# A two-layer hybrid decoder trunk: down product by column quarters, scatter in four row tiles, another order of the expert loads, other ends of the layers

## The chip, the cores and the metric

One Trainium2 chip, of which the kernel uses one core. The metric is the device time of one execution in microseconds (us), lower is better.

## The reference, cut to what matters

x is 256 tokens by 1024 features, float32. Each of two layers does a mixer and a mixture of experts (MoE), each on a normed input and added back. The change touches the MoE part, and the last norm.

```python
for layer in range(2):
    h = h + mixer(rms_norm(h, mix_norm))             # even: MoBA + RetNet heads; odd: dilated windows
    h = h + hier_moe(rms_norm(h, ffn_norm[layer]), ...)
return rms_norm(h, final_norm)

def hier_moe(h, ...):                                # 32 experts, 4 groups, top-1 group, top-2 inside it
    hid = jax.nn.silu(xb @ w_gate[e]) * (xb @ w_up[e])    # w_gate[e], w_up[e]: 1024 x 512
    y = hid @ w_down[e]                                    # w_down[e]: 512 x 1024
    out = zeros((n_tok, d)).at[row_tok].add(y * row_gate[:, None])
```

Every expert is computed: 3 matrices of 2 MB each, 32 experts, 2 layers. With the mixers' weights the kernel reads 439.72 MB.

## The kernel before, in words

**Memory.** `ring` holds ten units of 2 MB, filled by SyncE's queue (SP) alone. Four pairs of units (`PAIR_AT`) hold gate and up weights, two (`DOWN_AT`, units 9 and 6) down weights. During a layer's mixer the units hold the blocks of the input projection (0 to 5), and unit 6 the split weights (`split`), 7 the keys (`kT`), 8 the queries (`qT`) and `h_high`, 9 and 6 the output projection (`W_OUT_AT`).

**The MoE stage.** Expert e has 32 slots. I call its steps on TensorE G(e), D(e), S(e). `gather` brings the tokens of four experts to their slots with one-hot matmuls. `gate_up` (L836, G) makes 32 matmuls of 256 columns on four column tiles into bank 6. ScalarE takes the exponential and a copy, VectorE does `hidden` (L1267: SiLU, product, transpose to `hidT`). `down` (L855, D) turns the gates, then makes 8 matmuls of 512 columns: column tile j holds the product of hidden features j, so the four partial products stand in four groups of 32 partitions of banks 4 and 5. ScalarE copies bank 4 (L603) and VectorE bank 5 (L1293) to `y_sb`. `scatter` (L873, S) is 4 full matmuls of 512 columns, which add the partial products, weight them and add them to the four accumulator banks 0 to 3. `start_sums` puts h into these banks.

**Order.** TensorE runs, for each expert e: G(e+2), D(e), S(e), and after S of every second expert of a group `gather` for the next group. Groups of four experts, seven of them in a loop, the last one behind it as code of its own. (A further round for experts with more than 32 tokens stands between, under an `If`.) SP runs `load_group` (L401): wait for G(e), load pair e+4 (P(e+4)), wait for D(e), load down weights e+2 (W(e+2)). The queue is in order, so P(e+5) is asked for only when D(e) is done.

**Between the layers.** After the last scatter ScalarE and VectorE copy h back, TensorE turns it (`turn_h`), ScalarE and VectorE split it in a high and a low part (`split_hT`, `split_columns`), and `project` begins with the weights that `split_chunks` has split.

**The end.** After the last scatter, per token tile t: squares on ScalarE (L724), variance on VectorE, power on GpSimd, one Newton step, two multiplications with gain (L1401), output DMA.

## Time and profile before

| | |
|---|---|
| runs | 1209.9, 1211.75, 1213.74 us; median 1211.75 |
| profiled execution | 1207.12 us; its span 1204.7 us |
| TensorE busy | 980.2 us (81%) |
| VectorE, ScalarE, GpSimd busy | 420.7, 231.0, 36.9 us |
| DMA | 441.34 MB, mean 366 GB/s |
| the chain that ended last | DMA 43%, PE 41%, DVE 9%, ACT 3%, issue 2% |

PE is TensorE, PEld its weight loads, DVE VectorE, ACT ScalarE, POOL GpSimd, SPq the queue of SyncE. A float32 matmul stands in the trace as two records, so "x8" is four matmuls. Times in a timeline are us from the start of the span. "[1.85 <-DVE ...]" is the idle time of the engine before the row and what ended it.

### The profile page before, as it was taken

The numbers are of one execution on the slowest core, as the hardware profiler recorded it, in microseconds if no ns is written. First come the engines' busy times: TensorE is split into PE (matmuls) and PEld (weight loads), VectorE is DVE, ScalarE is ACT, GpSimd is POOL, SyncE is SP. The second block draws the span as 40 slices with busy tenths as digits, with TensorE's granted clock in tenths as the row PEclk, the third lists the DMA queues.
The fourth block names the chain that finished last, engine by engine and source line by source line (L and its number), as shares of the span: only waits on it lengthen the run. The fifth ranks groups of instructions, "written<-read, shape, count | busy, mean of one in ns | idle before, by whom it ended". The sixth has DMA issues, their size and how long they took to land.

```text
span 1204.7 us, 18458 instructions
## 1 busy us (share of the span) xinstructions
PE 980.2 (81%) x7528; PEld 535.0 (44%) x7528; DVE 420.7 (35%) x1073; ACT 231.0 (19%) x553; POOL 36.9 (3%) x52
## 2 busy tenths in 40 slices
PE   8998998878787768676899999888877768777865
PEld 6874544434342424342378656344343434343422
DVE  6774533232222222222278735322322222222222
ACT  5643111010000000000255630101100000000001
POOL 1002000000000000000010210000000000000000
PEclk9999999998999999998999998999999999899999
DMA  9976369999999999999895543799999999999993
GB/s 359 304 283 271 140 272 428 430 427 428 429 429 429 428 428 429 429 428 424 341 338 232 223 163 135 302 428 427 429 429 429 427 428 430 429 428 427 430 425 160
DMA packets 50681, 441.34 MB, mean 366 GB/s; under 512 B 8784, under 2 KB 8784, under 8 KB 25936
## 3 DMA queue, kind: packets, MB, share of 16 engines
q1 hardware_dynamic: 50496, 440.26, 88.2%
q8 instruction: 27, 0.44, 0.1%
q10 hardware_dynamic: 144, 0.52, 0.1%
q14 instruction: 14, 0.11, 0.0%
HBM read 439.72 MB, written 1.05 MB: 366 GB/s over the span
## 4 chain that ended last, share of the span: by engine, by line
DMA 43%; PE 41%; DVE 9%; ACT 3%; issue 2%; SPq 1%; POOL 1%; DVEq 0%; ACTq 0%
DMA ring<-in_w_expert_up 32%; PE bank L848 12%; DMA ring<-in_w_expert_down 11%; PE bank L880 6%; PE bank L905 4%; PE bank L867 3%; PE bank L756 3%; PE bank L758 3%; PE bank L757 3%; PE bank L830 2%; DVE work L1273 1%; DVE work L1293 1%; PE bank L733 1%; PE bank L938 1%; DVE split L1073 1%
## 5 line engine op out<-in xcount | busy, mean ns | idle before, releaser
L848 PE MATMUL bank<-ring,work 128*32 128x256 f32 x4096 | 264.4, 415 | 82.2 <-DMA ring<-in_w_expert_up 71.4
L880 PE MATMUL bank<-work 128*128 128x512 f32 x512 | 235.0, 601 | 95.6 <-DVE work L1293 95.6
L848 PEld LDWEIGHTS bank<-ring,work 128*32 128x32 f32 x4096 | 146.5, 119 | 209.2 <-issue 108.6
L1272 DVE TENSOR_SCALAR work<-work 128x128 f32<-128x128 f32 x64 | 14.5, 227 | 538.3 <-ACT work L596 538.3
L880 PEld LDWEIGHTS bank<-work 128*128 128x128 f32 x512 | 92.0, 189 | 243.7 <-issue 243.7
L595 ACT ACTIVATE work<-bank 128x128 f32<-128x128 f32 x64 | 17.8, 278 | 684.4 <-PE bank L848 684.4
L867 PE MATMUL bank<-ring,work 128*32 128x512 f32 x1024 | 123.1, 598 | 16.1 <-DMA ring<-in_w_expert_down 16.1
L756 PE MATMUL bank<-split,h_high 128*128 128x512 f32 x192 | 77.2, 402 | 6.8 <-DVE split L1073 3.4
L1073 DVE SCALAR_TENSOR_TENSOR split<-ring,gains,split 128x512 fp32r<-128x512 f32 x96 | 68.0, 748 | 24.1 <-ACT split L635 23.4
L758 PE MATMUL bank<-split,h_high 128*128 128x512 f32 x192 | 75.0, 391 | 0.0
L757 PE MATMUL bank<-split,h_low 128*128 128x512 f32 x192 | 74.9, 390 | 0.0
L635 ACT ACTIVATE split<-ring,gains 128x512 fp32r<-128x512 f32 x96 | 65.9, 720 | 28.0 <-PE bank L758 27.5
L830 PEld LDWEIGHTS bank<-work,xn 128*128 128x128 f32 x512 | 59.5, 192 | 9.1 <-issue 9.1
L1273 DVE RECIPROCAL work<-work 128x128 f32<-128x128 f32 x64 | 61.0, 953 | 2.2
L830 PE MATMUL bank<-work,xn 128*128 128x128 f32 x512 | 59.9, 275 | 0.8 <-DVE work L1245 0.8
L603 ACT COPY work<-bank 128x512 f32<-128x512 f32 x64 | 37.5, 586 | 105.5 <-PE bank L867 105.5
L905 PE MATMUL bank<-ring,hT 128*128 128x512 f32 x128 | 57.1, 596 | 0.0
L867 PEld LDWEIGHTS bank<-ring,work 128*32 128x32 f32 x1024 | 27.6, 109 | 65.8 <-issue 56.0
L1262 DVE TENSOR_TENSOR work<-bank,gains 128x512 f32<-128x512 f32 x32 | 22.1, 691 | 96.2 <-PE bank L830 96.2
L1293 DVE COPY work<-bank 128x512 f32<-128x512 f32 x64 | 43.8, 685 | 23.8 <-PE bank L867 23.8
L756 PEld LDWEIGHTS bank<-split,h_high 128*128 128x128 f32 x192 | 36.0, 188 | 17.3 <-DVE h_low L1065 6.2
L758 PEld LDWEIGHTS bank<-split,h_high 128*128 128x128 f32 x192 | 36.0, 188 | 7.9
(144 smaller groups left out, 691.8 us busy)
## 6 DMA issues: line engine op xcount, KB each, us to landing
ring<-in_w_expert_gate SPq DMA_DIRECT2D x64, 2048.0 KB, 30.6
ring<-in_w_expert_up SPq DMA_DIRECT2D x64, 2048.0 KB, 35.0
ring<-in_w_expert_down SPq DMA_DIRECT2D x64, 2048.0 KB, 26.3
ring<-in_w_in_even SPq DMA_DIRECT2D x5, 2048.0 KB, 18.3
ring<-in_w_in_odd SPq DMA_DIRECT2D x5, 2048.0 KB, 20.9
ring<-in_w_out_even SPq DMA_DIRECT2D x2, 2048.0 KB, 8.6
ring<-in_w_out_odd SPq DMA_DIRECT2D x2, 2048.0 KB, 14.3
ring<-in_w_in_even SPq DMA_DIRECT2D x2, 1024.0 KB, 8.2
```

Source lines behind the costliest of these rows:

```text
L635: act.activation(w_high[u % PARTS], ring[:, j, 512 * c:512 * c + 512], ACT.Copy, scale=gains[:, 2 * l, c:c + 1]).then_inc(w_high_ready, 1)
L756: pe.matmul(bank, high, wh, start=(c == 0), stop=False)
L757: pe.matmul(bank, low, wh, start=False, stop=False)
L758: last = pe.matmul(bank, high, wl, start=False, stop=(c == C - 1))
L830: last = pe.matmul(psum[4 + c // 4][:, P * (c % 4):P * (c % 4) + P], xn_c[:, t, c, :], onehot[:, t, :, :].rearrange("p k s -> p (k s)"), s ...
L848: last = pe.matmul(psum[6][32 * j:32 * j + 32, 0:2 * P].rearrange("p (a s) -> p a s", a=2), xT[:, c, SLOTS * k:SLOTS * k + SLOTS], ring[:, ...
L867: last = pe.matmul(psum[4 + half][32 * j:32 * j + 32, :], hidT[k][:, 32 * j:32 * j + 32], ring[:, DOWN_AT[k % 2], D * j + 512 * half:D * j ...
L880: pe.matmul(acc[t][half][:, :], gatedT[:, P * t:P * t + P], y_sb[:, 512 * half:512 * half + 512], start=False, stop=last).then_inc(scatter ...
L905: last = pe.matmul(mix_bank(n, t)[:, :], oT[:, c, P * t:P * t + P], ring[:, W_OUT_AT[n], 512 * c:512 * c + 512], start=(c == MIX_ORDER[l][ ...
L1073: dve.scalar_tensor_tensor(out=w_low[u % PARTS], in0=ring[:, j, 512 * c:512 * c + 512], scalar=gains[:, 2 * l, c:c + 1], in1=w_high[u % PA ...
L1273: chain.link(dve.reciprocal(eb, eb))
L1293: dve.tensor_copy(y_sb[:, 512:1024], psum[5][:, :]).then_inc(y_high[l], 1)
```

## The change

The down product: all four tiles q hold the same hidden features j in turn and add over j in the bank; tile q makes output columns 256q to 256q+255. So y is 128 partitions by 256 columns (32 slots for each quarter), in bank 4 alone. ScalarE alone copies it. The scatter makes 8 matmuls of 256 columns, each with 32 rows of the array (`tile_position=(32 * q, 0)`), quarter q into bank q. `gather` stands ahead of the scatter. `start_sums` stands ahead of the MoE stage, in the place of three warm-up matmuls, and no longer between G(1) and G(2). SP asks for P(4) and P(5) first, then W(2), W(3), and then in the old order. Units change: split weights in 7, keys in 6, second half of the output projection in 7; the loads before the MoE stage follow. Between the layers the first two chunks of layer 1's weights are split before the wait for the last scatter, h is copied back in quarters once both token tiles are done, and turned through banks 4 to 7. At the end both token tiles go together.

```diff
-W_OUT_AT = DOWN_AT
+W_OUT_AT = (9, 7)
+SPLIT_AT, KT_AT, QT_AT = 7, 6, 8
+QUARTER = D // 4
...
-        y_sb = work[:, 4096:5120]
-        acc = [[psum[2 * (1 - t) + half] for half in range(2)] for t in range(T)]
+        y_sb = work[:, 4096:4352]
+        acc = [psum[q][:, :].rearrange("p (t n) -> p t n", t=T) for q in range(4)]
...
-                load_pair(l, l * EXPERTS + GE - 1, GE - 1)
-                for k in range(2):
-                    sp.wait_ge(mixed[l], T * (k + 1))
-                    load_down(l, l * EXPERTS + k, k)
+                sp.dma_start(ring[:, unit + 1, :], up_rows[row]).then_inc(pair_arrived[l][GE - 1], 16)
+                load_down(l, l * EXPERTS + 1, 1)
+                sp.wait_ge(mixed[l], T)
+                load_down(l, l * EXPERTS, 0)
+                sp.wait_ge(mixed[l], T * 2)
+                sp.dma_start(ring[:, unit, :], gate_rows[row]).then_inc(pair_arrived[l][GE - 1], 16)
...
-                with sp.Fori(0, GROUPS_OF - 1) as g:
-                    load_group(l, 0, g)
+                for e in range(2):
+                    next_pair(l, e, e + GE, e)
+                for e in range(2):
+                    next_down(l, e, e + AHEAD, e)
+                load_rest(l, 0)
...
+            def load_rest(l, r):
+                with sp.Fori(0, GROUPS_OF - 2) as g:
+                    for k in range(GE):
+                        e = GE * g + AHEAD + k
+                        next_pair(l, r * EXPERTS + e, GE * g + (AHEAD + GE + k), (AHEAD + k) % GE)
+                        next_down(l, r * EXPERTS + e, GE * g + (2 * AHEAD + k), k % 2)
+                for e in range(EXPERTS - 6, EXPERTS - 4):
+                    next_pair(l, r * EXPERTS + e, e + 4, e % GE)
+                    next_down(l, r * EXPERTS + e, e + 2, e % 2)
...
-                act.copy(y_sb[:, 0:512], psum[4][:, :]).then_inc(y_low[l], 1)
+                act.copy(y_sb, psum[4][:, 0:QUARTER]).then_inc(y_ready[l], 1)
...
-                for half in range(2):
-                    for j in range(4):
+                for j in range(4):
+                    for q in range(4):
                         last = pe.matmul(
-                            psum[4 + half][32 * j:32 * j + 32, :], hidT[k][:, 32 * j:32 * j + 32],
-                            ring[:, DOWN_AT[k % 2], D * j + 512 * half:D * j + 512 * half + 512],
-                            start=True, stop=True, tile_position=(0, 32 * j))
+                            psum[4][32 * q:32 * q + 32, 0:QUARTER], hidT[k][:, 32 * j:32 * j + 32],
+                            ring[:, DOWN_AT[k % 2], D * j + QUARTER * q:D * j + QUARTER * q + QUARTER],
+                            start=(j == 0), stop=(j == 3), tile_position=(0, 32 * q))
...
                 for t in range(T):
-                    for half in range(2):
-                        pe.matmul(acc[t][half][:, :], gatedT[:, P * t:P * t + P], y_sb[:, 512 * half:512 * half + 512],
-                                  start=False, stop=last).then_inc(scattered[l], 1)
+                    for q in range(4):
+                        rows = slice(32 * q, 32 * q + 32)
+                        last = pe.matmul(acc[q][:, t, :], gatedT[rows, P * t:P * t + P], y_sb[rows, :],
+                                         start=False, stop=last_expert and t == T - 1, tile_position=(32 * q, 0))
+                last.then_inc(scattered[l], 1)
...
                     down(l, r, g, k)
-                    scatter(l, expert_no(r, g, k), not after and k == GE - 1)
                     if k == GE - AHEAD - 1 and after:
+                        pe.wait_ge(y_ready[l], e + 1)
                         gather(l, group_no(*after))
+                    scatter(l, e, not after and k == GE - 1)
...
-                keep_warm(2, cst[:, 0:512])
+                for q in range(2):
+                    start_sums(q)
...
-                keep_warm(1, cst[:, 0:512])
+                for q in range(2, 4):
+                    start_sums(q)
...
-                start_sums(l)
...
+                if l < LAYERS - 1:
+                    act.wait_ge(gain_loaded[2 * l + 2], 16)
+                    split_chunks(l + 1, 0, 0, AHEAD)
+                act.wait_ge(scattered[l], (more + 1) * EXPERTS)
+                if l < LAYERS - 1:
+                    for q in range(2):
+                        act.copy(h[:, :, QUARTER * q:QUARTER * q + QUARTER], acc[q]).then_inc(h_left_back, 1)
+                else:
+                    for q in range(4):
+                        if q >= 2:
+                            act.wait_ge(gained, q - 1)
+                        for t in range(T):
+                            act.activation(h[:, t, QUARTER * q:QUARTER * q + QUARTER], acc[q][:, t, :],
+                                           ACT.Square, accum_out=sq4[:, t, q:q + 1]).then_inc(squared, 1)
+                    act.wait_ge(rstd_ready, T * (2 * LAYERS + 1))
+                    act.wait_ge(gained, 4)
+                    act.activation(xn_t[:, 0, :], xn_t[:, 0, :], ACT.Copy, scale=rstd[:, 0:1]).then_inc(out_ready[0], 1)
```

VectorE likewise splits two chunks and copies quarters 2 and 3 of h; at the end it multiplies each quarter with the gain (`gained`), adds the eight sums, does one Newton step for both tiles, and scales tile 1.

## Rows read from the trace of the kernel before

**Rows 1.** The page: 40 slices of the span, in tenths.

```profile
PEclk9999999998999999998999998999999999899999
DMA  9976369999999999999895543799999999999993
```

**Rows 2.** The page's costliest groups: busy us, mean ns of one; idle before.

```profile
L848 PE MATMUL bank<-ring,work 128*32 128x256 f32 x4096 | 264.4, 415 | 82.2 <-DMA ring<-in_w_expert_up 71.4
L880 PE MATMUL bank<-work 128*128 128x512 f32 x512 | 235.0, 601 | 95.6 <-DVE work L1293 95.6
```

**Rows 3.** Windows: both MoE starts; last columns are granted clock, DMA share, GB/s.

```profile
165.00:170.00 5.00, 4.53 (x62) 1.75 (x54) 1.82 (x5) 1.22 (x4) 0.00 (x0) 1.00 0.51 216
170.00:175.00 5.00, 3.60 (x8) 1.44 (x9) 1.25 (x3) 0.18 (x1) 0.00 (x0) 1.00 0.86 308
...
765.00:770.00 5.00, 4.80 (x66) 1.92 (x58) 1.60 (x4) 0.95 (x4) 0.00 (x0) 1.00 0.57 242
770.00:775.00 5.00, 3.34 (x8) 1.44 (x8) 1.48 (x4) 0.45 (x1) 0.00 (x0) 1.00 0.81 279
```

**Rows 4.** Timeline of the SP queue, layer 0's second request (W(2)).

```profile
169.73 0.33 SPq L384 DMA_DIRECT2D ring<-in_w_expert_down  x1
```

**Rows 5.** Timeline of TensorE, start of layer 0's MoE stage.

```profile
142.95 3.66 PE L733 MATMUL bank<-cst 128*128 128x512 f32 x4
...
148.36 3.81 PE L830 MATMUL bank<-work,xn 128*128 128x128 f32 x32 [0.45 <-DVE work L1245]
...
160.01 3.70 PE L887 MATMUL bank<-h,cst 128*128 128x512 f32 x8
163.64 3.66 PE L848 MATMUL bank<-ring,work 128*32 128x256 f32 x64
```

**Rows 6.** Timeline of TensorE, last experts of layer 0.

```profile
558.16 1.57 PE L848 MATMUL bank<-ring,work 128*32 128x256 f32 x18 [3.86 <-issue]
563.64 4.05 PE L848 MATMUL bank<-ring,work 128*32 128x256 f32 x46 [3.91 <-issue]
...
571.75 3.67 PE L880 MATMUL bank<-work 128*128 128x512 f32 x8 [1.83 <-DVE work L1293]
...
579.31 1.92 PE L867 MATMUL bank<-ring,work 128*32 128x512 f32 x16
...
596.39 3.67 PE L880 MATMUL bank<-work 128*128 128x512 f32 x8 [0.91 <-DVE work L1293]
```

**Rows 7.** Timeline of TensorE, layer 1: one wait in the loop, then its end.

```profile
1111.75 5.35 PE L848 MATMUL bank<-ring,work 128*32 128x256 f32 x64 [3.36 <-DMA ring<-in_w_expert_up]
...
1162.18 1.50 PE L848 MATMUL bank<-ring,work 128*32 128x256 f32 x24 [1.66 <-issue]
...
1192.40 3.67 PE L880 MATMUL bank<-work 128*128 128x512 f32 x8 [0.91 <-DVE work L1293]
```

**Rows 8.** The chain: start, us; P(30) of layer 0 and of layer 1.

```profile
519.89 35.95 DMA ring<-in_w_expert_up
...
1120.53 35.33 DMA ring<-in_w_expert_up
```

**Rows 9.** DMA issues at 581 to 582 us (W(31), first half block); us to landing.

```profile
ring<-in_w_expert_down SPq DMA_DIRECT2D x1, 2048.0 KB, 7.9
ring<-in_w_in_odd SPq DMA_DIRECT2D x1, 1024.0 KB, 10.2
```

**Rows 10.** Timelines of ScalarE and VectorE: copy to gatedT, between the layers, the end.

```profile
568.25 0.39 ACT L601 COPY work<-bank 128x256 f32<-128x256 f32 x1
...
599.72 2.56 ACT L635 ACTIVATE split<-ring,gains 128x512 fp32r<-128x512 f32 x4
...
602.79 2.48 DVE L1065 TENSOR_TENSOR h_low<-bank,h_high 128x512 fp32r<-128x512 f32 x4 [0.68 <-ACT h_high L617]
...
1200.28 1.41 DVE L1401 SCALAR_TENSOR_TENSOR xn<-bank,small,hT 128x512 f32<-128x512 f32 x2
```

More of the change, by code:

```diff
@@ L292, in build @@
         squared = sem("squared")
+        gained = sem("gained")
+        out_ready = sems("out_ready", T)
         var_ready = sem("var_ready")
@@ L422, in load_w_out @@
+            def load_across(l, r):
+                for k in range(6):
+                    next_pair(l, r * EXPERTS + k - GE, k, k % GE)
+                    next_down(l, r * EXPERTS + k - GE, EXPERTS - AHEAD + k if k < AHEAD else k - AHEAD, k % 2)
             def load_w_out(l, n):
@@ L871, in down, with scatter @@
                 last.then_inc(down_done[l], 1)
-            def scatter(l, e, last):
+            def scatter(l, e, last_expert):
                 pe.wait_ge(gatedT_ready[l], e + 1)
-                pe.wait_ge(y_low[l], e + 1)
-                pe.wait_ge(y_high[l], e + 1)
+                pe.wait_ge(y_ready[l], e + 1)
                 for t in range(T):
-                    for half in range(2):
-                        pe.matmul(acc[t][half][:, :], gatedT[:, P * t:P * t + P], y_sb[:, 512 * half:512 * half + 512],
-                                  start=False, stop=last).then_inc(scattered[l], 1)
@@ L883, in start_sums @@
-            def start_sums(l):
-                for t in range(T):
-                    for half in range(2):
-                        pe.matmul(acc[t][half][:, :], ident, h[:, t, 512 * half:512 * half + 512],
-                                  start=True, stop=False).then_inc(scattered[l], 1)
+                    for q in range(4):
+                        rows = slice(32 * q, 32 * q + 32)
+                        last = pe.matmul(acc[q][:, t, :], gatedT[rows, P * t:P * t + P], y_sb[rows, :],
+                                         start=False, stop=last_expert and t == T - 1, tile_position=(32 * q, 0))
@@ L890, in group, with start_sums @@
+                last.then_inc(scattered[l], 1)
+            def start_sums(q):
+                pe.matmul(acc[q], ident, h[:, :, QUARTER * q:QUARTER * q + QUARTER], start=True, stop=False)
             def group(l, r, g, after):
                 for k in range(GE):
+                    e = expert_no(r, g, k)
                     if k < GE - AHEAD:
@@ L1298, in group @@
                         choose_slots(l, group_no(*after), GE * after[1])
+                    if k < GE - AHEAD or after:
+                        hidden(l, e + AHEAD, ahead)
+                    if k == GE - AHEAD - 1 and after:
                         columns(l, group_no(*after))
@@ new lines, in _ @@
+                    split_chunks(l + 1, 0, 0, AHEAD)
+                dve.wait_ge(scattered[l], (more + 1) * EXPERTS)
+                if l < LAYERS - 1:
+                    for q in range(2, 4):
+                        dve.tensor_copy(h[:, :, QUARTER * q:QUARTER * q + QUARTER], acc[q]).then_inc(h_right_back, 1)
+            link = norm_link
+            squares = 4 * 2 * LAYERS
+            dve.wait_ge(fin_loaded, 16)
+            for q in (2, 3, 0, 1):
+                if q < 2:
+                    dve.wait_ge(squared, squares + T * (q + 1))
+                cols = slice(QUARTER * q, QUARTER * q + QUARTER)
+                dve.tensor_tensor(xn_t[:, :, cols], acc[q], gain_row[:, cols].unsqueeze(1).broadcast_to([P, T, QUARTER]),
+                                  ALU.mult).then_inc(gained, 1)
```

118 lines of the change are left out of this document (52 added, 66 removed).

## The prediction

> **What bounds the kernel now.** I read the page first. The row of the DMA engines stands at 9 tenths in both MoE stages, while PE's share is lower there than in the mixers [rows 1]. The costliest groups then say how PE waits: G, the largest, had 71.4 us of idle time ended by the DMA of up weights, but S 95.6 us by VectorE's copy of y [rows 2]. The reader should see two kinds of time in this. While the DMA queue is full, an expert costs its bytes: three transfers of 2048 KB are 6.29 MB, at about 429 GB/s [rows 1] 14.7 us, whatever PE does. PE needs less: G 3.64 us (its row less the overlap with the next), the gates' turn 0.37, D 1.90, the wait 1.83, S 3.67, and a quarter of a gather of 3.8 [rows 5, 6], together 12.4. So the 235 us of S are mostly slack. What PE does sets the time in three places alone: (a) where the queue runs dry after a MoE stage's start, (b) from the last pairs' landing to the stage's end, (c) behind the last scatter. The mixers, from `project` to the gather, are untouched but for loads that move.
>
> **(a) The start.** The windows show the hole: behind P(4) the 16 DMA engines move 216 and then 308 GB/s, in layer 1 242 and 279 [rows 3]. Against 429 this is 2.5 + 1.4 = 3.9 us without data, in layer 1 2.2 + 1.7 = 3.9. It ends when W(2) is asked for at 169.73 us [rows 4], since SP waits for D(0) before it looks at G(1). After the change P(5) is asked for when G(1) ends, at about 160.0 us, where now `start_sums` begins [rows 5]. P(4) transfers for 9.8 us, until about 167.5, so the hole closes; W(2) is then asked for at about 167 (G(2), turn, D(0) without the 3.70 of `start_sums` ahead), and P(5) covers until 177. The stream gains 3.9 us in each layer. The price: four matmuls of 0.92 us replace three of warm-up ahead of the gather, one more, of which the gather's idle 0.45 us [rows 5] hides half. +0.5. Net -3.4 us on every landing of the stage. Waits of SP further on have the old order, the landing order of P and W at the end is unchanged. The moved loads at the end of a mixer have the same bytes behind the same waits, except gate(3), which is asked for last; G(3) comes after some 20 us, so nothing.
>
> **The steps of an expert.** D: 16 matmuls of 256 columns on four tiles. G makes 32 of these in 3.64 us, so 1.82, against 1.90 [rows 5, 6]: I keep 1.90. The wait between D and S: VectorE's `hidden` and copy are out of it, what is left is ScalarE's copy of 256 columns, 0.39 us [rows 10], with its handing over 0.63, against 1.83 (0.91 where no `hidden` stands ahead [rows 6, 7]). S: eight matmuls of 256 columns and 32 rows. No row tiles are in the trace. Lower bound: G's rate on column tiles, 0.114 us each, 0.91. Upper bound: no overlap, eight times 0.46, 3.67 as now. A middle one: a weight load of 128 columns with its matmul record comes every 0.12 us in the gather (32 in 3.81 us [rows 5]), 16 of them 1.9. I take 1.3, between the ends that the overlap on column tiles makes likely.
>
> The Trainium skill (TensorE: Matmul & The Clock Gate, packing of small matmuls) gives 3.07 times for four row tiles of 512 columns, which would make S 3.67 / 3.07 = 1.2 us, an estimate from that page, and the sum below 0.2 us better; no row here shows it.
>
> **(b) The end of layer 0's stage.** Before: P(30) lands at 555.8 [rows 8], P(31) three transfers later, 570.6, W(29) one more, 575.4. G(30) runs 558.2 to 567.7, 6.2 us of it stalled as "issue" behind the loop's exit [rows 6]; D(28) ends at 569.9, S(28) at 575.4, D(29) at 581.2, S(31) at 600.1. After, step by step: P(30) 552.4, G(30) ends 564.3 with the same stalls, D(28) 566.6, S(28) 566.6 + 0.63 + 1.3 = 568.5 (P(31) is there since 567.2), G(31) 572.1, D(29) 574.4. Now W(31), asked for at 574.5, is what is late next: before it took 7.9 us [rows 9], and 600 us was far behind. It lands at 582.4 (W(30) at 576.9, S(30) over by 580.8). D(31) 584.3, S(31) 584.3 + 0.63 + 1.3 = 586.2. That is 13.9 us earlier.
>
> Then the turn to layer 1. The split of two chunks is put ahead of the wait; it needs the first half block, which lands 10.2 us after its issue [rows 9], 0.4 us after that of W(31): 585.1. ScalarE splits until 586.6 (four took 2.56 us [rows 10]), VectorE until 587.4, and copies two quarters of h by 588.8, where the scatter alone would allow 587.7. Turn of the first bank 0.6, cast 0.6, four subtractions 2.48 [rows 10] with handings over: `project` at 592.7, before 605.3. Of the 13.9 us 12.6 are left. The mixer behind it keeps its length; its blocks stand in the queue at 5.4 us each against 11.6 us of projection each.
>
> **(b) in layer 1**, in the clock of before: P(30) 1155.9 [rows 8] becomes 1152.5, G(30) with its stall of 1.66 us [rows 7] ends 1160.3 instead of 1163.7, D(28) 1162.6, S(28) 1164.5. P(31) lands at 1167.0, so PE waits; G(31) 1167.6 to 1171.2, W(29) 1171.9, D(29) 1173.9. W(31) 8.3 us later, 1182.3, D(31) 1184.2, S(31) 1186.1, before 1196.1 [rows 7]. -10.0.
>
> **(c) The end.** Before, 8.6 us from the last scatter to 1204.7: two squares 1.3, the root 2.9 with the other tile's two multiplications in it, two multiplications 1.41 [rows 10], output 3.0. After: eight squares of 256 columns 2.8; the root without the 1.41 but with sums of four, 1.8; one scaling of 1024 columns 1.05; the second output's issue 0.4 behind the first; 3.0. 9.05, so +0.5. Here the change loses; bounds 8.1 (squares at 0.25 each) to 10.1 (0.39 each).
>
> **Sum.** -12.6 - 10.0 + 0.5 = -22.1 us. Span 1204.7 to 1182.6; the execution's own time 1207.1 to 1185.0. The median of the runs is 4.6 us above the profiled one, so 1211.75 - 22.1 = 1189.6.
>
> **Rivals.**
>
> 1. *Row tiles don't overlap.* S keeps 3.67. Layer 0: S(28) 570.9, G(31) 574.5, D(29) 576.8, S(29) 581.1, D(30) 583.4, S(30) 587.7, D(31) 590.0, S(31) 594.3, and no block to wait for, so `project` at 599.8: -5.5. Layer 1 the same way: D(28) 1162.6, S(28) 1166.9, G(31) 1171.2, D(29) 1173.5, S(31) 1191.0: -5.1. With the end -10.1: 1201.6. For it: no row shows row tiles. Against: column tiles overlap fully, G at 0.114 us a matmul.
> 2. *The stream's hole or the tail gives back less*: stalls behind the loop's exit are longer (the code of a group grows by 96 matmul records and as many loads), or W(30) and W(31) land later. One stall of 3.9 us [rows 6] more in each layer, one half of it hidden by the wait for P(31) in layer 1: -16, 1195.8.
> 3. *The slow clock, the other side.* After 3.36 us of waiting G took 5.35 us instead of 3.64 [rows 7], so the clock fell to 1.2 GHz when PE waited. Now PE waits longer: an expert needs 3.64 + 0.37 + 1.90 + 0.63 + 1.3 + 0.9 = 8.7 us of 14.7, and one gap is near 6 us. If all ran at 1.2 GHz, the 8.1 us of work would double: 16.8 us, above the 14.7 of the bytes, and each of some 25 experts in each layer would cost 2.1 us more: +105 - 22, about 1295. It decides from the point where over three quarters of PE's work (6.0 of 8.1) is slow. Against it: the busier PE gets, the more clock it was granted, and down to three quarters nothing is lost in the loop. In the tail no gap is over 2.5 us. The Trainium skill (TensorE: Matmul & The Clock Gate, the HAM clock gate) says that the clock is throttled by default and activity releases it, and warns of waits between bursts. By that rule, the clock rows above agree, but the page leaves the share open.
> 4. *Nothing is gained*: the hole moves behind P(5) and S is hidden anyway, within 3.6 us. Against: the tail's 14 us of scatters stand on the chain with no cover.
>
> **How the numbers follow.** The forecast 0.63, rival 1 0.13, rival 2 0.12, rival 3 0.06, rival 4 0.06. The forecast's own range: S between 0.91 and 1.9 us moves two scatters in each layer, -1 and +2; the end ±1; the tail's waits ±2; the spread of runs ±2: 1184 to 1194. To leave out no more than 2 in 10 it must reach rivals 1 and 2: 1184 to 1202. What a measurement of this kernel can tell is about 0.3%, 3.6 us. Faster by more than that is the forecast and rivals 1 and 2, 0.88; within it rival 4, 0.05; slower rival 3 and a rest, 0.07.
>
> **What would show it.** (a) No dip below 420 GB/s in the 20 us behind the first P(4), and pairs 4 and 5 asked for 4 us apart. Scatter groups of 16 records in 0.9 to 1.8 us, 0.6 us behind D. PE idle before G for 5 to 6 us in the loop, DMA still at 427 to 430 GB/s, clock lower than 0.97 in the mean. (b) In both tails D(31) is released by the DMA of down weights, `project` starts about 12 us earlier. (c) 9 us from the last scatter to the end. The prediction is wrong if S takes 3.6 us, if the rate falls in the stages, or if D(31) waits much longer than 8 us behind D(29).

## The result, and the profile after

The changed kernel takes 1194.68 us (median of 4 runs, 1193.59 to 1195.5). The kernel before took 1210.91 us in the same job (4 runs, 1209.9 to 1213.74). The ratio is 0.9862, 95% interval 0.9842 to 0.9881: 16.2 us faster, where 22.1 were forecast. The profiled execution took 1195.5 us with a span of 1193.5, 11.2 less than before's 1204.7. The medians lie further apart than the profiles because before's profiled execution (1207.12 us) was quicker than all of its timed runs, and after's was the slowest of its four. What follows compares spans, and so explains 11.2 us against 22.1.

The page of after, 40 slices: the granted clock, the DMA share and GB/s.

```profile
PEclk9999898878787888786899998988797978787877
DMA  9967369999999999999995543899999999999994
GB/s 359 308 272 289 141 265 424 428 429 429 428 429 429 428 428 428 428 429 426 381 379 231 217 165 136 349 427 430 429 428 427 429 429 428 428 428 429 428 425 171
```

The same row of the page of before, where the 429 GB/s of the prediction stand:

```profile
GB/s 359 304 283 271 140 272 428 430 427 428 429 429 429 428 428 429 429 428 424 341 338 232 223 163 135 302 428 427 429 429 429 427 428 430 429 428 427 430 425 160
```

The rate in both MoE stages is the one of before: the bytes still set the time of the loop. The clock row is new against [rows 1]: 7 and 8 in the stages, mean 0.865 against 0.966. TensorE waits more, and is granted less. The costliest groups of after say the same of G, D and S (busy us, mean ns; idle before):

```profile
L878 PE MATMUL bank<-ring,work 128*32 128x256 f32 x4096 | 318.3, 478 | 226.6 <-DMA ring<-in_w_expert_up 208.5
...
L897 PE MATMUL bank<-ring,work 128*32 128x256 f32 x2048 | 126.1, 387 | 17.9 <-DMA ring<-in_w_expert_down 17.9
L910 PE MATMUL bank<-work 32*128 32x256 f32 x1024 | 74.3, 403 | 29.1 <-ACT work L622 29.1
```

Against [rows 2], S fell from 235.0 us to 74.3 and its wait from 95.6 to 29.1. G grew from 264.4 to 318.3 and its wait for up weights from 71.4 to 208.5. TensorE has 160.7 us less to do in S and waits 66.5 less ahead of it; of this 227 us, 191 came back as a slower G (53.9) and a longer wait for the same up weights (137.1).

**The start of layer 0.** Windows of after (columns: PE, PEld, DVE, ACT, POOL, clock, DMA share, GB/s), then SP's queue:

```profile
165.00:170.00 5.00, 4.89 (x86) 2.50 (x76) 3.60 (x11) 0.86 (x4) 0.00 (x0) 1.00 1.02 433
170.00:175.00 5.00, 4.53 (x80) 2.75 (x80) 1.39 (x4) 0.32 (x1) 0.00 (x0) 1.00 1.00 423
...
770.00:775.00 5.00, 5.00 (x68) 4.01 (x70) 1.71 (x3) 0.00 (x0) 0.00 (x0) 1.00 0.98 416
```

```profile
158.99 0.33 SPq L387 DMA_DIRECT2D ring<-in_w_expert_gate  x1
...
163.31 0.33 SPq L387 DMA_DIRECT2D ring<-in_w_expert_gate  x1
...
169.95 7.88 SPq L391 DMA_DIRECT2D ring<-in_w_expert_down  x2
```

The windows that had 216 and 308 GB/s in layer 0 and 242 and 279 in layer 1 [rows 3] have over 415. Pairs 4 and 5 are asked for 4.3 us apart. From the first gather (151.60; before 148.36 [rows 5]) to P(31)'s landing, 569.90 as the chain below has it, it is 418.3 us. Before it was 570.6 - 148.36 = 422.2. So the hole's 3.9 us are gained in full, but the gather itself started 3.2 us later.

**The end of layer 0's stage**, timeline of TensorE, and two lines of the chain:

```profile
570.03 5.35 PE L878 MATMUL bank<-ring,work 128*32 128x256 f32 x64 [2.13 <-DMA ring<-in_w_expert_up]
...
578.20 1.15 PE L910 MATMUL bank<-work 32*128 32x256 f32 x16 [0.58 <-ACT work L622]
...
586.65 3.17 PE L897 MATMUL bank<-ring,work 128*32 128x256 f32 x32 [2.90 <-DMA ring<-in_w_expert_down]
590.38 1.23 PE L910 MATMUL bank<-work 32*128 32x256 f32 x16 [0.56 <-ACT work L622]
593.73 3.50 PE L769 MATMUL bank<-cst,h 128*128 128x128 f32 x16 [2.12 <-DVE h L1421]
598.62 0.50 PE L786 MATMUL bank<-split,h_high 128*128 128x512 f32 x1 [1.40 <-DVE h_low L1096]
```

```profile
533.63 36.27 DMA ring<-in_w_expert_up
...
577.68 8.83 DMA ring<-in_w_expert_down
```

S is 1.15 us instead of 3.67 [rows 6], 0.58 behind D. D(31) waits for W(31), as forecast. But G(31), D(31) and the turn stand behind waits and run slow: 5.35, 3.17 and 3.50 us. Warm, G takes 3.66 and D 1.93 in this same trace, and the turn 2.01 in one of the runs below.

**The end of layer 1** in the chain of after, then the last work of ScalarE and the output's issue:

```profile
1145.97 1.99 issue
1147.96 2.77 PE bank L878 x20
1150.74 2.60 issue
1153.34 4.68 PE bank L878 x44
...
1167.86 8.98 DMA ring<-in_w_expert_down
...
1176.98 3.02 PE bank L897 x32
...
1180.54 2.12 PE bank L910 x16
```

```profile
1182.69 0.38 ACT L751 ACTIVATE h<-bank 128x256 f32<-128x256 f32 x1 [2.29 <-PE bank L910]
...
1187.95 1.15 ACT L755 ACTIVATE xn<-xn,small 128x1024 f32<-128x1024 f32 x1 [2.24 <-DVE small L1440]
```

```profile
1189.13 0.82 SPq L497 DMA_DIRECT2D out<-xn  x2
```

The tail of layer 1 has the same form. The last scatter ends at 1182.63, and the end takes 10.87 us, where it took 8.6.

Stretch by stretch, from the traces:

| stretch | before | after | change | forecast |
|---|---|---|---|---|
| turn of tile 1 to gather, layer 0 | 10.22 | 13.56 | +3.3 | +0.5 |
| gather to last scatter, layer 0 | 451.70 | 440.01 | -11.7 | -14.4 |
| last scatter to `project` | 5.27 | 7.01 | +1.7 | +1.3 |
| `project` to gather, layer 1 | 143.31 | 143.76 | +0.4 | +0.5 |
| gather to last scatter, layer 1 | 447.43 | 440.25 | -7.2 | -10.5 |
| last scatter to the end | 8.63 | 10.87 | +2.2 | +0.5 |

The sum is -11.3, within 0.1 of the spans. Of the -11.7 us of layer 0's stage 3.9 are the hole of the start and 7.8 the tail; of the -7.2 of layer 1's stage it is 3.6 and 3.6 (P(30) landed 407.2 us behind the gather before, 403.6 after).

How far can a stretch of one profile be trusted? Four traces have the same code in the stage of layer 1, and it took 437.94, 440.25, 441.39 and 442.50 us (`copy_first`, after, `start_warm`, `end_by_tile`). In layer 0 four such traces took 439.23 to 440.74 us. So a difference of a stage that is inside these spreads says nothing by itself, and the miss between two medians can't be split by stretches at all.

### The profile page after: what moved, and what is told of

It is laid out like the page before. It is cut to its first block, busy times and chain, and to the rows that moved or that the text cites. A ratio compares the mean times of both kernels' runs of the same rounds, so it can differ in the third digit from the quotient of the medians.

```text
span 1193.5 us, 21386 instructions
## 1 busy us (share of the span) xinstructions
PE 879.7 (74%) x9052; PEld 543.0 (45%) x9052; DVE 384.9 (32%) x1006; ACT 218.9 (18%) x562; POOL 36.3 (3%) x51
## 3 DMA queue, kind: packets, MB, share of 16 engines
HBM read 439.72 MB, written 1.05 MB: 369 GB/s over the span
## 4 chain that ended last, share of the span: by engine, by line
DMA 56%; PE 34%; DVE 4%; ACT 2%; issue 2%; SPq 1%; POOL 1%; POOLq 0%; ACTq 0%; DVEq 0%
DMA ring<-in_w_expert_up 40%; DMA ring<-in_w_expert_down 16%; PE bank L878 9%; PE bank L897 5%; PE bank L935 4%; PE bank L786 3%; PE bank L788 3%; PE bank L787 3%; PE bank L916 1%; PE bank L968 1%; DVE split L1104 1%; PE bank L860 1%; PE bank L837 1%; DVE work L1113 1%; POOL work L548 1%
## 5 line engine op out<-in xcount | busy, mean ns | idle before, releaser
L878 PE MATMUL bank<-ring,work 128*32 128x256 f32 x4096 | 318.3, 478 | 226.6 <-DMA ring<-in_w_expert_up 208.5
L878 PEld LDWEIGHTS bank<-ring,work 128*32 128x32 f32 x4096 | 162.9, 136 | 376.2 <-issue 268.4
L897 PE MATMUL bank<-ring,work 128*32 128x256 f32 x2048 | 126.1, 387 | 17.9 <-DMA ring<-in_w_expert_down 17.9
L910 PE MATMUL bank<-work 32*128 32x256 f32 x1024 | 74.3, 403 | 29.1 <-ACT work L622 29.1
L897 PEld LDWEIGHTS bank<-ring,work 128*32 128x32 f32 x2048 | 61.2, 110 | 63.2 <-DMA ring<-in_w_expert_down 16.3
L910 PEld LDWEIGHTS bank<-work 32*128 32x128 f32 x1024 | 49.4, 186 | 54.6 <-issue 52.5
L622 ACT COPY work<-bank 128x256 f32<-128x256 f32 x64 | 23.8, 372 | 110.0 <-PE bank L897 110.0
L787 PEld LDWEIGHTS bank<-split,h_low 128*128 128x128 f32 x192 | 36.1, 188 | 6.9
L1293 DVE TENSOR_TENSOR work<-bank,gains 128x512 f32<-128x512 f32 x32 | 22.1, 691 | 49.1 <-PE bank L860 49.1
```

The source lines that it names most:

```text
L622: act.copy(y_sb, psum[4][:, 0:QUARTER]).then_inc(y_ready[l], 1)
L787: pe.matmul(bank, low, wh, start=False, stop=False)
L878: last = pe.matmul(psum[6][32 * j:32 * j + 32, 0:2 * P].rearrange("p (a s) -> p a s", a=2), xT[:, c, SLOTS * k:SLOTS * k + SLOTS], ring[:, ...
L897: last = pe.matmul(psum[4][32 * q:32 * q + 32, 0:QUARTER], hidT[k][:, 32 * j:32 * j + 32], ring[:, DOWN_AT[k % 2], D * j + QUARTER * q:D * ...
L910: last = pe.matmul(acc[q][:, t, :], gatedT[rows, P * t:P * t + P], y_sb[rows, :], start=False, stop=last_expert and t == T - 1, tile_posit ...
```

## The experiments

Each run stands beside the kernel before in its job. "after" is the changed kernel.

**Which part gives what.** `order_alone`: the kernel before with the new order of SP alone (its units, product and scatter unchanged).

```diff
                 load_first(l)
-                with sp.Fori(0, GROUPS_OF - 1) as g:
-                    load_group(l, 0, g)
+                for e in range(2):
+                    next_pair(l, e, e + GE, e)
+                for e in range(2):
+                    next_down(l, e, e + AHEAD, e)
+                load_rest(l, 0)
```

> The kernel before with one thing changed, the order in which SP asks for the experts' weights (pairs 4 and 5 first). Theory: the hole of 3.9 us behind pair 4 closes in each layer, and since PE's tail hangs on the landing of pair 30 in both layers, all of it comes back: about 7 to 8 us faster than before, 1203 to 1204. Rival (the start is hidden by what comes later): 0 to 2 us.

1208.5 us (10 runs) against 1209.42 (13), ratio 0.9975 (0.9954 to 0.9996); span 1207.5. Windows of this run:

```profile
165.00:170.00 5.00, 5.00 (x55) 2.34 (x57) 2.48 (x6) 0.00 (x0) 0.00 (x0) 1.00 1.00 426
...
185.00:190.00 5.00, 3.35 (x8) 1.63 (x9) 1.80 (x5) 0.45 (x1) 0.00 (x0) 1.00 0.95 357
...
200.00:205.00 5.00, 3.51 (x8) 1.44 (x8) 1.31 (x3) 0.36 (x1) 0.00 (x0) 1.00 0.84 297
```

The first hole is closed and two new ones stand behind it, at 185 and 200 us, together (1 - 357/429) x 5 + (1 - 297/429) x 5 = 2.4 us: the requests that wait for D(1) come late. D(1) ends 32.5 us behind the gather here, and 25.8 in after. P(30) lands 406.0 us behind the gather instead of 407.5. This is rival 4's mechanism, and it holds for the order alone.

`order_undone`: after, with P(4), W(2), P(5), W(3) asked for in that order.

```diff
                 for e in range(2):
                     next_pair(l, e, e + GE, e)
-                for e in range(2):
                     next_down(l, e, e + AHEAD, e)
```

> The changed kernel with the old order of requests (pair 4, down 2, pair 5, down 3). With `start_sums` gone from between G(1) and G(2), the hole is only about 1.5 to 2.5 us (D(0) ends 6.4 us behind G(1), pair 4 alone transfers for 9.8 us from G(0) on). Theory: 1 to 2.5 us slower per layer than the changed kernel, 3 to 5 in all, 1198 to 1200. Rival (the new order is worth its full 3.9 us in each layer here too): 8 us slower, 1203.

1198.94 us (4 runs), ratio 0.9883 (0.9837 to 0.993); span 1196.9. Windows:

```profile
165.00:170.00 5.00, 4.42 (x74) 2.52 (x76) 2.90 (x7) 1.18 (x4) 0.00 (x0) 1.00 0.90 324
170.00:175.00 5.00, 4.62 (x80) 2.31 (x70) 1.66 (x4) 1.13 (x4) 0.00 (x0) 1.00 0.96 390
```

A hole of 1.7 us is left, and P(31) lands 420.0 us behind the gather, against 422.2 before and 418.3 after. So the rest of the change without the order closes about half of the hole. In layer 0's start that is not the faster scatter: W(2) waits for D(0), ahead of which no scatter stands, and D(0) ends 18.3 us behind the gather instead of 21.2, since `start_sums` is gone from between G(1) and G(2).

What does the order need beside it? Two runs further down take one thing away each. In `sums_back` `start_sums` stands between G(1) and G(2) again, and the scatters are fast; in `scatter_padded` a scatter with what is put behind it takes 4.0 us, but `start_sums` stays ahead and the wait between D and S is 0.58 us. P(31) lands 418.3 us behind the gather in the one and 418.2 in the other, as in after, and no window from 165 to 215 us is under 416 GB/s in either. The order needs an earlier D(1) than the kernel before has, and either of the two gives it; the fast scatter isn't needed for it.

**Does the speed of S count in the loop?** `scatter_padded`: after, with three full matmuls (2.84 us) behind every scatter.

```diff
                 last.then_inc(scattered[l], 1)
+                keep_warm(3, cst[:, 0:512])
```

> The changed kernel with three full matmuls of 512 columns (2.8 us) behind every scatter, into a bank that nobody reads then, so that a scatter costs about as much PE time as before. Theory: in the loop it is hidden, only the last scatters count: in each layer D(31) moves from the landing of W(31) to PE's own chain, 1 to 4 us later, and the padding behind the last scatter adds up to 2.8 in layer 0; a warmer clock gives 1 to 3 us back. In all 2 to 9 us slower, 1197 to 1204. Rival (the short scatter gives its gain in every expert): 64 x 2.5 = over 100 us slower. Rival (the clock is worth more than the scatter): no slower, 1190 to 1195.

1195.28 us (4 runs), ratio 0.9867 (0.9826 to 0.9907); span 1192.8, mean clock 0.960. In effect S lasts 4.0 us for each of 64 experts, and nothing is lost: in the loop it is hidden. In the tail the padding costs 2.8 us a scatter and buys the clock: D(31) takes 1.93 us in both layers, and G(31) 3.66 in layer 0 (5.29 in layer 1), and the stages are as long as in after (440.1, 440.7). So it does not show what the speed of S is worth in the tail: what the pads cost there, the clock gave back. No run here sets the speed of S in the tail apart from the clock. What shows it is the timeline: before, from G(31) on, TensorE hardly waited for a transfer, and the four scatters of 3.67 us with their waits stood in its chain [rows 6]; after, D(31) waits for W(31).

`scatter_serial`: after, with the eight matmuls of S in another order, the two of a row tile behind each other.

```diff
-                for t in range(T):
-                    for q in range(4):
+                for q in range(4):
+                    for t in range(T):
```

> The changed kernel with the scatter's eight matmuls in the order tile 0 twice, tile 1 twice, and so on, in the place of tiles 0 to 3 and again 0 to 3. In the changed kernel they take 1.15 us together. Theory (four row tiles run at a time, one tile's own matmuls one behind the other, all in order): five steps of 0.43 in the place of two, 2.1 to 2.4 us a scatter. Rival (the order doesn't count, the array takes any of them side by side): 1.15. The whole: 1 to 3 us more.

One execution, 1189.69 us, span 1187.7. The timeline in the loop:

```profile
311.52 1.17 PE L910 MATMUL bank<-work 32*128 32x256 f32 x16 [0.58 <-ACT work L622]
```

1.17 us against 1.15. I had expected over 2 us. That expectation fell: eight matmuls on four row tiles overlap as well in this order. The whole time, of a single execution, says nothing more.

**The cold tail.** `warm_tail`: three full matmuls into the idle bank 5 ahead of the wait for W(31), both layers.

```diff
                 pe.wait_ge(hidT_ready[l], e + 1)
+                if warm:
+                    for _ in range(warm):
+                        pe.matmul(psum[5][:, :], cst[:, 0:P], cst[:, 0:512], start=True, stop=True)
                 pe.wait_ge(down_arrived[l][k % 2], ...)
```

> The changed kernel with three full matmuls (2.8 us) ahead of the wait for W(31) in the last group, in both layers, into a bank that nobody reads then. Theory of the clock: PE waits 2.9 and 2.5 us for W(31) and then runs D(31) in 3.2 and 3.0 us instead of 1.9, the last scatter in 2.1 instead of 1.15, the turn of h in 3.5 instead of 2.2. Filled, these are at the full clock: 2 to 2.5 us faster in each layer, 4 to 5 in all, about 1190. Rival (the clock falls for what PE did earlier than this wait, or the filling delays D(31)): 0 to 1 us, or slower.

1194.01 us (4 runs), ratio 0.9858 (0.9817 to 0.9899), the time of after within its interval; span 1189.3. Both D(31) take 1.93 us and both S(31) 1.15, and the stages 438.4 and 438.9 us instead of 440.0 and 440.3. The first is below all four stages of that code, the second inside their spread. In layer 0 the gain does not arrive: last scatter to `project` is now 8.61 us. The chain of this run:

```profile
575.11 12.00 DMA ring<-in_w_in_odd
587.19 0.73 ACT split L654
...
590.78 3.63 PE bank L769 x16
```

ScalarE waits with its split for the first half block, which lands at 587.1, as the last scatter ends. This is the limit that the prediction named, with 12.0 us from issue to landing instead of its 10.2; in after the half block took 11.2 us and landed 0.6 us before the slow D(31) ended.

The length of the wait does not decide whether D(31) is slow. Layer 1 of `order_undone`, then of `scatter_serial`:

```profile
1180.69 3.56 PE L896 MATMUL bank<-ring,work 128*32 128x256 f32 x32 [1.50 <-DMA ring<-in_w_expert_down]
```

```profile
1173.20 1.93 PE L897 MATMUL bank<-ring,work 128*32 128x256 f32 x32 [1.53 <-DMA ring<-in_w_expert_down]
```

In all traces with the new scatter 16 D(31) stand behind a wait of 1.5 to 3.9 us with nothing put in: 15 took 2.6 to 3.6 us, and this one took 1.93. The five with full matmuls ahead of them (both layers here and in `scatter_padded`, layer 0 of `combined`) all took 1.93. So the filling holds the clock up, and what the low clock costs in layer 1 can be read without any edit: in `scatter_serial`, where D(31) and S(31) are warm, the stage took 437.38 us, 2.9 less than in after.

`copy_first`: after, with VectorE's split of two chunks moved behind its copy of h.

```diff
-                    split_chunks(l + 1, 0, 0, AHEAD)
                 dve.wait_ge(scattered[l], (more + 1) * EXPERTS)
                 ...
                         dve.tensor_copy(...).then_inc(h_right_back, 1)
+                    split_chunks(l + 1, 0, 0, AHEAD)
```

> The changed kernel, but VectorE copies its two quarters of h back before it splits the first two chunks of layer 1's weights. In the changed kernel VectorE splits until 592.4 and copies until 593.6 while the last scatter was over at 591.6 and ScalarE's copies at 592.7. Theory: the turn of h starts 0.8 us earlier, the mixer too, and the two splits (1.4 us) then stand in the gap before the subtractions: 0.5 to 0.9 us faster. Rival: they delay the subtractions by as much, 0.

1193.22 us (4 runs), ratio 0.9859 (0.9817 to 0.9902); span 1191.7. Last scatter to `project` 5.38 us, with this turn:

```profile
593.75 2.01 PE L769 MATMUL bank<-cst,h 128*128 128x128 f32 x16 [1.50 <-DVE h L1420]
```

TensorE waits 1.50 us for h instead of 2.12, and the turn ran warm. Neither is certainly the edit: the wait was 1.49 in `early_down` and 1.50 in `scatter_serial` too, which have VectorE's old order, but where VectorE was through with the split when the last scatter ended. The time is that of after within its interval.

`early_down`: in layer 1 no block of a next layer needs the ring. W(30) and W(31) go to free units as soon as G(28) is done.

```diff
+                        sp.wait_ge(gate_up_done[l], more * EXPERTS + EXPERTS - GE + 1)
+                        sp.dma_start(ring[:, e % 2, :], down_rows[...]).then_inc(early_arrived[e % 2], 16)
```

> The changed kernel, but in layer 1 the last two down matrices go to units 0 and 1, free since G(28), and are asked for behind W(29) without waiting for D(28) and D(29). In the changed kernel W(31) is asked for when D(29) ends, at 1167.9, and lands 9.0 us later at 1176.9. Theory (the tail hangs on that request): the stream has no break, W(31) lands about 1.5 to 2.5 us earlier and the end with it, 1192.2 to 1193.2. Rival (the bytes alone set it): 0.

1192.88 us (4 runs), ratio 0.9855 (0.9813 to 0.9897), the time of after within its interval; span 1191.0. Stage 1 is 437.49 us instead of 440.25, but 437.94 and 437.38 were seen without the edit too (`copy_first`, `scatter_serial`). The timeline:

```profile
1149.76 2.78 PE L883 MATMUL bank<-ring,work 128*32 128x256 f32 x20 [7.92 <-issue]
1155.30 5.34 PE L883 MATMUL bank<-ring,work 128*32 128x256 f32 x44 [2.76 <-issue]
...
1176.44 1.93 PE L907 MATMUL bank<-ring,work 128*32 128x256 f32 x32
```

D(31) waits for nothing and is warm: the wait for W(31) is gone, and what that is worth in time isn't shown. What bounds the tail now is TensorE's own chain behind the two stalls of G(30).

`no_rounds_pe`: after, without TensorE's code for further rounds (which never runs with these inputs), so that no branch stands behind the loop.

```diff
-                pe.wait_ge(rounds_ready[l], 1)
-                more = pe.value_load(rounds_i[0:1, l:l + 1], min_val=0, max_val=MAX_ROUNDS - 1)
-                with pe.If(more > 0):
-                    ...
-                group(l, more, GROUPS_OF - 1, None)
+                group(l, 0, GROUPS_OF - 1, None)
```

> The changed kernel with TensorE's code for further rounds of the experts left out (with these inputs no expert has more than 32 tokens, and it is branched over), so that the last group's code follows its loop directly. In all kernels so far G(30), the first work behind the loop, stands as 'issue' for 2 to 8 us and, but for layer 0 in some, again in its middle for 2 to 4.7. Theory (it is the code behind a far branch that has to come while the DMA engines are full): the stalls shrink to under 1 us. In layer 0 the wait for P(31) takes most of the gain, in layer 1 S(28) is over before P(31) lands and D(31) moves by 1 to 2 us: 1 to 3 us faster. Rival (the stall belongs to the loop's exit itself or to the fetch of any new code): unchanged.

1195.27 us (4 runs), ratio 0.9859 (0.9816 to 0.9903); span 1194.3. The timeline has G(30) and G(31) of layer 1:

```profile
1146.58 6.12 PE L878 MATMUL bank<-ring,work 128*32 128x256 f32 x64 [5.77 <-DMA ring<-in_w_expert_up]
...
1161.28 5.61 PE L878 MATMUL bank<-ring,work 128*32 128x256 f32 x64 [4.61 <-DMA ring<-in_w_expert_up]
```

G(30) is in one piece, released by its data, in both layers. With the branch G(30) of layer 1 was interrupted by a stall in every trace but that of `scatter_padded`. So the stalls very likely belong to the skipped branch, as far as one trace without it can show. The stages are no shorter than in after (442.1 and 440.3), and the time is that of after. TensorE is simply earlier, waits longer for P(31), and runs G(31) cold, so no cost of the stalls is to be seen in after that the wait for P(31) and W(31) would not have had.

**The start and the end.** `sums_back`: `start_sums` is put back between G(1) and G(2), with the three warm-up matmuls.

```diff
-                for q in range(2):
-                    start_sums(q)
+                keep_warm(2, cst[:, 0:512])
...
                 gate_up(l, 0, 0, 1)
+                for q in range(4):
+                    start_sums(q)
```

> The changed kernel with `start_sums` back between G(1) and G(2) and the three warm-up matmuls ahead of the gather. It asks why layer 0's MoE stage began 3.2 us later than before (gather at 151.60 instead of 148.36). Theory of the clock: both programs are the same up to the logits, and it was half clock from 140.4 us on that stretched them (3.6 us instead of 2.0), by chance of where the drop falls, so the start moves by chance here too and the sums' place costs or gives 0.5 us a layer: 1193 to 1197. Rival (the moved sums cost the 3 us): gather back at 148.4 to 149, and up to 3 us faster if the later D(0) costs nothing: 1191 to 1192.

1191.11 us (4 runs), ratio 0.9844 (0.9801 to 0.9886); span 1189.4. Turn to gather is 10.11 and 11.86 us, the stages 439.5 and 439.6. With the fast scatters, moving `start_sums` ahead gains nothing that these times show, and it costs 0.2 to 0.4 us of start (12.10 against 11.86 in layer 1, 10.46 in six traces against 10.11 in layer 0).

`start_warm`: one full matmul in the gap ahead of the second tile's logits.

```diff
                 turn_mixed(l, 1)
+                keep_warm(1, cst[:, 0:512])
                 logits(l, 1)
```

> The changed kernel with one full matmul of 512 columns in the 1.18 us that TensorE waits ahead of the second tile's logits, in both layers. The clock falls to half there, at 140 to 144 us, and stays so for 6 to 10 us; in seven traces the gather of layer 0 then starts anywhere from 148.1 to 152.3. Theory (the small products of 36 and 32 columns and the gaps let it fall, one more full product holds it up): gather at 147.5 to 148.5 in layer 0 and 0.5 to 1.5 us shorter from turn to gather in layer 1: 1 to 4 us faster. Rival (it falls all the same, for the rest is as thin as before): 0, or 0.2 us slower.

1191.4 us (4 runs), ratio 0.9825 (0.9783 to 0.9867); span 1191.7. Windows of after, then of this run:

```profile
141.00:144.00 3.00, 3.00 (x16) 3.00 (x16) 0.00 (x0) 0.00 (x0) 0.00 (x0) 0.50 0.91 377
...
147.00:150.00 3.00, 3.00 (x8) 1.80 (x7) 2.02 (x7) 0.00 (x0) 1.11 (x4) 0.50 0.00 0
```

```profile
141.00:144.00 3.00, 2.28 (x13) 1.46 (x13) 2.13 (x7) 1.10 (x5) 0.54 (x1) 1.00 0.83 257
...
147.00:150.00 3.00, 2.42 (x9) 1.12 (x8) 2.76 (x13) 0.48 (x3) 0.00 (x0) 1.00 0.07 27
```

In after the clock stands at 0.50 (1.2 GHz) for 9 us ahead of the gather, although TensorE is never idle there; with one matmul more it is 1.00, and turn to gather takes 10.10 and 10.09 us in the two layers. In the traces without it, whose code up to the gather is that of after, layer 0 took 10.45 to 10.47 six times, and 12.13, 13.56 and 13.57. In the program of before it took 10.22, and 12.70 in `order_alone`. So some 3.1 of after's +3.3 us are where the clock happened to fall, and 0.2 the change's price. The one matmul is no guarantee: in layer 1 of `combined`, which has it too, four matmuls of `start_sums` took 3.57 us instead of 1.96, and turn to gather 10.46.

```profile
732.06 3.57 PE L930 MATMUL bank<-h,cst 128*128 128x512 f32 x4
```

`end_by_tile`: after, with the end per token tile as before, in quarters.

```diff
-                    for q in range(4):
-                        ...
-                        for t in range(T):
+                    for t in range(T):
+                        for q in range(4):
                             act.activation(h[:, t, ...], acc[q][:, t, :], ACT.Square, ...)
```

> The changed kernel with the end per token tile as in the kernel before (squares of tile 0, then of tile 1, root and multiplication with gain per tile, first output while the second tile is still worked on). The changed end took 10.85 us from the last scatter, before 8.6. Theory: the two outputs of 0.5 MB that leave together cost 1.4 us more than one behind the other, so this end takes about 9.2 to 9.8 us: 1 to 1.6 us faster, 1193 to 1193.7. Rival (the joint work on both tiles is the better): 0 to 1 us slower.

1193.46 us (4 runs), ratio 0.9857 (0.9816 to 0.9897); span 1192.2. Last scatter to the end 10.91 us, as in after. That the joint end is what costs fell. Eight squares of 256 columns stand behind the last scatter in either form. The scatter before did tile 0 first and tile 1 last, and the trace of before shows tile 0's squares starting under it, 1.7 us ahead of its end at 1196.07:

```profile
1194.39 0.60 ACT L724 ACTIVATE xn<-bank 128x512 f32<-128x512 f32 x1 [2.24 <-PE bank L880]
```

So only tile 1's two squares (1.3 us) stood behind the scatter, where now all eight do (3.0). A scatter of 1.15 us can't give such a cover. That this is the loss is read from the rows; no run brings the cover back.

**All repairs together.** `combined`: `start_warm`, copies of h ahead of the split on both engines, `warm_tail` in layer 0 with one full matmul ahead of the turn, `early_down`, and the outputs stored by two engines' queues.

```diff
+                    act.wait_ge(out_ready[0], 1)
+                    act.dma_start(out[0, 0:P, :], xn_t[:, 0, :]).then_inc(out_stored, 16)
```

> The changed kernel with what the other runs point to, all in one: a full matmul ahead of the second logits in both layers (as in start_warm), h copied back before the two chunks are split on both engines (as in copy_first), three full matmuls ahead of the wait for W(31) in layer 0 (as in warm_tail) and one ahead of the turn of h, W(30) and W(31) of layer 1 asked for early (as in early_down), and the two output tiles stored by the queues of two engines. Theory that the losses of the changed kernel stand one behind the other on one path, so that each repair adds: turn to gather 10.1 us in both layers (13.6 and 12.1 in the changed kernel's profile, some 2 of the 3.5 in layer 0 a matter of chance), stage 0 at 438.4 (440.0), last scatter to project 5.4 (7.0), stage 1 437.5 or less (440.3), the end 10.4 (10.9); the span 8 to 10 us shorter than 1193.5, so 1184 to 1187 for the time. Rival, that the repairs cover one another (the split chunks need the first half block, which lands late whatever TensorE does; W(31) lands when the queue is through): last scatter to project stays at 6.5 to 8.6, stage 1 at 440, and the time is that of the single repairs, 1189 to 1192.

1187.51 us (5 runs, 1185.21 to 1188.78) against 1210.41 (9 runs), ratio 0.9805 (0.9776 to 0.9834); span 1185.5. Of the expected stretches the starts (10.10, 10.46), stage 1 (437.43) and the end (10.44) came, last scatter to `project` nearly (5.65 instead of 5.4), and stage 0 did not: 440.12 instead of 438.4. The chain and the timeline:

```profile
575.03 9.60 DMA ring<-in_w_expert_down
```

```profile
584.68 1.93 PE L911 MATMUL bank<-ring,work 128*32 128x256 f32 x32 [1.06 <-DMA ring<-in_w_expert_down]
```

D(31) is warm, but W(31) landed 9.60 us behind D(29), where it took 8.83 in after, 9.80 in `order_undone` and at most 8.8 in `warm_tail`. Why it varies by 1 us is open. The last 0.4 us of the end are not due to the two queues: from the first issue to the end it is 4.3 us (4.4 in after), but tile 1's output, ready first, no longer waits in the queue behind tile 0's.

This version is 22.9 us faster than before, and its interval lies below that of after, which no single repair's does. So together they gain; how much each gives is not shown by times (`start_warm` had the lowest ratio, 0.9825). Both theories missed, by 0.5 and 1.5 us: the time lies between their ranges, nearer to the sum.

## Why the prediction was right, and which terms were off

The forecast's mechanism held but for the clock in the tails, and 1194.68 lies within the stated range of 1184 to 1202. It lies 0.7 above the forecast's own range of 1184 to 1194: that it is inside is owed to the width added for rivals 1 and 2, neither of which is what happened. By its steps:

- **(a)** held. No dip, P(4) and P(5) 4.3 us apart, the stream 3.9 us earlier against the gather in layer 0, and P(30) 403.6 us behind the gather in layer 1, from 407.2. What the step did not say is that the order alone only moves the hole (`order_alone`): it needs an earlier D(1) too, by the faster scatter (`sums_back`) or by the moved `start_sums` with the shorter wait (`scatter_padded`).
- **The steps of an expert** held: D 1.93 (1.90 forecast), the wait 0.58 (0.63), S 1.15 (1.3). 3.67 / 1.15 = 3.2 times. The Trainium skill (TensorE: Matmul & The Clock Gate, packing of small matmuls) has 3.07 times for four row tiles of 512 columns; the trace agrees, at 256 columns.
- **(b), layer 0**: S(31) ended at 591.6, forecast 586.2. The 5.4 us by the forecast's own chain: P(31) 2.7 later (the start); G(31) at the low clock, 1.7 longer, of which 1.1 fall into slack that the forecast had given away, 0.6; W(31) 8.83 behind D(29) instead of 7.9 or 8.0, 0.8; D(31) 1.3 longer. `project` came 7.0 behind S(31), forecast 6.5, for another reason than forecast: the half block, though it took 11.2 us instead of 10.2, was there, and the turn was cold (3.50) and stood behind VectorE's split, which ran after the last scatter.
- **(b), layer 1**: 440.25 us from gather to last scatter, forecast 437.0. Of the 3.3: D(29) came 0.7 late. G(30) ended 12.0 us behind P(30)'s landing instead of 7.8 (two stalls, and a low clock), and most of these 4.2 us lay where the forecast had TensorE wait for P(31). W(31) 8.98 instead of 8.3, 0.7; D(31) 1.2 and S(31) with its wait 0.7 longer at the low clock.
- **(c)** was mis-sized: 10.9 us, forecast 9.05, and above the bound of 10.1. Squares 3.0 (2.8), root 2.2 (1.8), scaling 1.15 (1.05), the two outputs 4.4 from issue to the end (3.4).
- **The start** came out at +3.3 instead of +0.5 in this profile, by chance (`start_warm`); in six of nine traces it would have been +0.2, and the medians need not contain it.

The wrong step is one sentence of rival 3: "In the tail no gap is over 2.5 us." It priced all of the tail at full clock. The gap ahead of D(31) was 2.90 us in layer 0, and D took 3.17; in layer 1 it was 2.47, and D took 3.00. Nor is a bound on the gap enough: D(31) took 3.56 us behind 1.50 in `order_undone`. The Trainium skill's rule (TensorE: Matmul & The Clock Gate, the HAM clock gate) that waits between bursts throttle the engine was cited for the loop, where it costs nothing, and not for the tail, where it does: with full matmuls in the gap D(31) took 1.93 us in both layers (`warm_tail`). Start 2.8, stage 0 2.7, hand-over 0.4, stage 1 3.3 and end 1.7 make the 10.9 us by which the span missed (to rounding). The gain between medians, 16.2 us, misses by 5.9, so a part of the span's miss is the choice of the two executions that were profiled.

Rival 1 is excluded (S 1.15), rival 3 too: the clock fell to 0.77 in the loop and G took up to 6.5 us, yet the rate stayed at 428. It was right that a faster kernel gets a slower engine. Rival 2's stalls were there, longer than forecast in layer 1, and cost nearly nothing (`no_rounds_pe`). Its time, 1195.8, was the nearest by number, but not for its reason. Rival 4 holds for the order alone, and not for the whole change, which is 16.2 us faster.

## What to carry to other kernels

When a change turns work into waiting on TensorE, price what stands behind each new wait at the low clock too, and ask of each such piece whether anything hides it: in a loop bound by DMA it is free, in a tail it stands on the chain, and a few matmuls into an idle bank ahead of the wait buy it back, unless a transfer comes just as late (`warm_tail`, layer 0). Reordering requests pays only if the engine that frees the buffers keeps up, so test the order with and without each part that makes it earlier. And before a stretch of one profile is laid to an edit, look at how much it varies between traces that share its code. Speeding up a step that lies under a transfer gives nothing except at the ends of the stage, and there the slow step may have been the cover for something else.

## What the runs showed of the hardware

- Four row tiles of 32 rows overlap: eight float32 matmuls of 256 columns in 1.15 us, whether neighbours use different tiles or the same one (1.17). Four full matmuls of 512 columns, the same work before, took 3.67.
- TensorE ran at clock 0.50 over 9 us in which it was busy all the time, on matmuls of 36, 32 and 512 columns, after 0.92 and 1.18 us of idle time. A full matmul in the second gap kept it at 1.00 in both layers of `start_warm` and in layer 0 of `combined`, but not in layer 1 of `combined`.
- A product that takes 1.93 us took 2.6 to 3.6 behind a wait of 1.5 to 3.9 us in 15 of 16 cases, and 1.93 in the 16th (1.53 us of wait) and in all five with full matmuls ahead of it.
- The clock makes copies of one program differ by 3.1 us in the 10 to 14 us ahead of the gather; a profile of one execution can carry such a difference into every stage behind it.
- TensorE stalled for 2.0 to 3.9 us, twice in after's layer 1 as in before's layer 0 [rows 6], on its way out of a loop past a branch that isn't taken; in `sums_back` one stall was 4.7. In the one trace with the branch's code gone the stalls were gone.
